# Prompt chunks of a hybrid decoder layer: K and V copies to the scalar engine, states read by row groups, and a shared centring

## What is computed

```python
u = rms_norm(h, norm_mix) @ w_in
y_ssd, y_ret, y_gla, y_lru = mixers(split(u))
h = h + concat([y_ssd, y_ret, y_gla, y_lru]) @ w_out
hn = rms_norm(h, norm_ffn)
h = h + (silu(hn @ w_gate) * (hn @ w_up)) @ w_down
```

## Time and profile before

| | |
|---|---|
| median of 3 runs | 1433.16 us (1429.13 to 1435.86) |
| the profiled execution | 1434.77 us |
| its span, first to last instruction | 1433.0 us |
| PE, share of the span busy | 97% |
| DVE | 46% |
| ACT | 34% |
| POOL | 29% |
| mean granted clock of PE | 0.984 of 2.4 GHz |

### The profile page before, as it was taken

One profiled execution on the slowest core, in us unless ns is written; L12 is line 12 of the kernel. 1 busy time (PEld: TensorE's weight loads), 2 busy tenths in 40 slices (PEclk: granted clock), 3 DMA queues, 4 the chain that ended last, 5 costly groups with the idle time before them and its releaser, 6 DMA issues.

```text
span 1433.0 us, 25769 instructions
## 1 busy us (share of the span) xinstructions
PE 1388.3 (97%) x11189; PEld 1339.7 (93%) x11189; DVE 654.6 (46%) x1280; ACT 489.6 (34%) x649; POOL 415.4 (29%) x205
## 2 busy tenths in 40 slices
PE   6998999999999999999999989999999999999996
PEld 6887888999999999999989878889999999999996
DVE  5744766364321333133756547755533223322334
ACT  5625344342221222122443263534322122222231
POOL 1100001333444444443511000014333333444441
PEclk9999999999999999999999999999999999999998
DMA  8644645223222222232446456332232223322231
GB/s 276 135 101 114 144 112 120 62 86 89 89 87 83 87 87 87 89 89 89 118 131 134 103 133 158 78 90 88 75 89 89 89 89 89 88 85 83 87 101 63
DMA packets 41345, 146.39 MB, mean 102 GB/s; under 512 B 5136, under 2 KB 6160, under 8 KB 41104
## 3 DMA queue, kind: packets, MB, share of 16 engines
q1 hardware_dynamic: 30528, 112.33, 26.6%
q0 software_dynamic: 6336, 23.07, 8.8%
q10 hardware_dynamic: 4368, 9.34, 2.1%
HBM read 136.68 MB, written 5.82 MB: 99 GB/s over the span
## 4 chain that ended last, share of the span: by engine, by line
PE 84%; DVE 7%; ACT 3%; DVEq 2%; DMA 2%; issue 1%; ACTq 1%; POOL 0%; SPq 0%
PE bank L1224 75%; DMA wl<-weights 1%; PE bank L1174 1%; PE bank L1453 1%; DMA tz<-rq 1%; PE bank L1345 1%; PE bank L1315 0%; ACT wh L403 0%; ACT wl L405 0%; PE bank L1190 0%; ACT xh L428 0%; PE bank L1459 0%; DVE h L1165 0%; PE bank L1185 0%; DVE ct L719 0%
## 5 line engine op out<-in xcount | busy, mean ns | idle before, releaser
L1224 PE MATMUL bank<-xh,wh 128*128 128x272 f32 x2208 | 653.2, 296 | 15.8 <-DVE xl L676 7.6
L1224 PE MATMUL bank<-xh,wl 128*128 128x272 f32 x2208 | 644.7, 292 | 0.0
L1224 PE MATMUL bank<-xl,wh 128*128 128x272 f32 x2208 | 641.3, 290 | 0.0
L375 POOL TENSOR_TENSOR wl<-raw,wh 128x1024 fp32r<-128x1024 f32 x157 | 377.1, 2402 | 594.4 <-ACT wh L403 578.5
L403 ACT ACTIVATE wh<-raw 128x1024 fp32r<-128x1024 f32 x199 | 210.8, 1060 | 688.4 <-PE bank L1224 665.8
L1224 PEld LDWEIGHTS bank<-xh,wh 128*128 128x128 f32 x2208 | 422.0, 191 | 23.3 <-issue 17.2
L1224 PEld LDWEIGHTS bank<-xl,wh 128*128 128x128 f32 x2208 | 422.5, 191 | 1.3 <-issue 0.5
L1224 PEld LDWEIGHTS bank<-xh,wl 128*128 128x128 f32 x2208 | 421.3, 191 | 0.0
L1143 DVE TENSOR_TENSOR tz<-bank,rs_bcast 128x272 f32<-128x272 f32 x176 | 77.5, 441 | 293.5 <-PE bank L1224 289.5
L1123 DVE TENSOR_TENSOR h<-h,bank 128x272 f32<-128x272 f32 x128 | 55.3, 436 | 215.5 <-PE bank L1224 215.5
L382 POOL DMA_DIRECT2D wl<-weights x44 | 38.1, 867 | 397.2 <-ACT wl L405 397.2
(11 more groups left out here) (360 smaller groups left out, 1790.5 us busy)
## 6 DMA issues: line engine op xcount, KB each, us to landing
raw<-weights SPq DMA_DIRECT2D x202, 512.0 KB, 3.6
wl<-weights POOLq DMA_DIRECT2D x44, 512.0 KB, 7.8
h<-x SPq DMA_DIRECT2D x4, 544.0 KB, 6.0
y<-h SPq DMA_DIRECT2D x4, 544.0 KB, 2.8
cs<-consts SPq DMA_DIRECT2D x1, 1656.5 KB, 9.3
rv<-rk ACTq DMA_DIRECT2D x8, 136.0 KB, 6.6
tz<-rq ACTq DMA_DIRECT2D x8, 136.0 KB, 4.0
S<-s_ssd ACTq DMA_DIRECT2D x2, 512.0 KB, 4.3
```

The source lines that it names most:

```text
L375: nc.gpsimd.tensor_tensor(wl[:, s, :], raw[:, s, :], wh[:, s, :].bitcast(F32), ALU.subtract).then_inc(lo_done, 1)
L1224: ins = mm(bank_, wt[:, n % RING, w], xx[:, cols], start=(i == 0 and j == 0), stop=(i == len(ks) - 1 and j == 2))
```

## The change

The masks `ssd_blocks`, `gla_blocks`, `ret_blocks` and the tile `dS` go (the table of constants loses 640 columns of 128 rows in float32). The states keep whatever K^T V has outside a head's block; PE reads only the own rows: per chunk from 1 on, four state matmuls in each mixer, of 64 x 64 tiles in SSD (before: four of 128 x 64) and retention (before: two of 128 x 128) and of 32 x 64 tiles in GLA (before: two of 128 x 128), all behind the four of V instead of between them. DVE adds K^T V from PSUM onto the state. ACT copies K of SSD, K and V of GLA, and V of retention, each with a new signal that PE's part b waits for. K of SSD is turned into M[1], V of retention into M[3], and GLA's output lies in M[2] and M[1], so `gla_a` now waits for ACT's copy of the chunk before (`gla_o`). DVE makes retention's `qt` before it waits for `ret_a`. In the centring ACT squares the two prompt halves from PSUM while DVE copies.

```diff
@@ signals
+        ssd_k, gla_kv, ret_v = (signal(n, 4) for n in ("ssd_k", "gla_kv", "ret_v"))
+        cent_mm, cent_first, cent_second, cent_out = (
+            signal(n, 1) for n in ("cent_mm", "cent_first", "cent_second", "cent_out"))
@@ scalar
                     a(D[:], M[0][:].rearrange("p (h i) -> p h i", h=4), ACT.Exp).then_inc(ssd_dx.sem, 1)
+                    a(K[:, 0:P], M[1][:, 384:512], ACT.Copy).then_inc(ssd_k.sem, 1)
+
+                def gla_a_(c):
+                    if c < SAMPLE:
+                        act.wait_ge(gla_a.sem, gla_a.at(layer, c + 1))
+                        a(V[:], M[1][:, 0:256], ACT.Copy)
+                        a(K[:, 0:P], M[1][:, 256:384], ACT.Copy).then_inc(gla_kv.sem, 1)
+                        gla_pre_(c + 1)
+
+                def ret_a_(c):
+                    if c < SAMPLE:
+                        act.wait_ge(ret_a.sem, ret_a.at(layer, c + 1))
+                        a(V[:], M[3][:, 256:512], ACT.Copy).then_inc(ret_v.sem, 1)
...
                 def ret_squares(_=None):
+                    act.wait_ge(cent_mm.sem, cent_mm.at(layer, 1))
+                    a(sq[:, 1, 0:SEQ], M[1][:], ACT.Square).then_inc(cent_second.sem, 1)
+                    act.wait_ge(cent_first.sem, cent_first.at(layer, 1))
+                    a(sq[:, 0, 0:SEQ], M[0][:], ACT.Square)
                     act.wait_ge(cent_out.sem, cent_out.at(layer, 1))
-                    squares(rv[:])
+                    a(sq[:, :, SEQ:TOK], rv[:, :, SEQ:TOK], ACT.Square).then_inc(n_sq.sem, 1)
@@ vector
-                    copy(K[:, 0:P], M[2][:, 384:512])
...
-                            stt(S_gla[:], S_gla[:], gla_last[:, c % 2, 0:1], dS[:], ALU.mult, ALU.add)
+                        new = M[3][:, 0:256]
+                        if c == 0:
+                            copy(S_gla[:], new)
+                        else:
+                            stt(S_gla[:], S_gla[:], gla_last[:, c % 2, 0:1], new, ALU.mult, ALU.add)
...
-                    copy(V[:], M[1][:, 0:256])
-                    copy(K[:, 0:P], M[1][:, 256:384])
...
                 def ret_a_(c):
                     _, off, n = CH[c]
+                    if c < SAMPLE:
+                        tt(qt[:, c % 2, :, :], rq[:, :, off:off + n], cst("ret_q").rearrange("p (t i) -> p t i", t=2), ALU.mult)
                     dve.wait_ge(ret_a.sem, ret_a.at(layer, c + 1))
...
-                    copy(V[:], M[2][:, 256:512])
-                    tt(qt[:, c % 2, :, :], rq[:, :, off:off + n], cst("ret_q").rearrange("p (t i) -> p t i", t=2), ALU.mult)
...
+                        for t in range(2):
+                            cols = slice(P * t, P * t + P)
+                            if c == 0:
+                                copy(S_ret[:, cols], M[0][:, cols])
+                            else:
+                                stt(S_ret[:, cols], S_ret[:, cols], cst("ret_last")[:, t:t + 1], M[0][:, cols],
                                     ALU.mult, ALU.add)
...
+                    copy(rv[:, 0, prompt], M[0][:]).then_inc(cent_first.sem, 1)
+                    copy(rv[:, :, sample], M[2][:, 0:2 * NS].rearrange("p (t n) -> p t n", t=2))
                     dve.drain().then_inc(cent_out.sem, 1)
+                    dve.wait_ge(cent_second.sem, cent_second.at(layer, 1))
+                    copy(rv[:, 1, prompt], M[1][:])
@@ tensor
+                    pe.wait_ge(ssd_k.sem, ssd_k.at(layer, c + 1))
                     for hd in range(4):
                         g, r = hd // 2, hd % 2
+                        mm(M[g][64 * r:64 * r + 64, 0:P], V[:, 64 * hd:64 * hd + 64], PT[:, hd, :], start=True, stop=c == 0)
+                    for hd in range(4 if c else 0):
+                        g, r = hd // 2, hd % 2
+                        rows = slice(64 * g, 64 * g + 64)
+                        mm(M[g][64 * r:64 * r + 64, 0:P], S_ssd[rows, 64 * hd:64 * hd + 64], qt[rows, c % 2, r, :],
+                           start=False, stop=True)
...
+                    if c:
+                        pe.wait_ge(gla_o.sem, gla_o.at(layer, c))
...
+                    pe.wait_ge(gla_kv.sem, gla_kv.at(layer, c + 1))
...
+                        rows = slice(32 * hd, 32 * hd + 32)
+                        mm(M[2 - t][64 * e:64 * e + 64, 0:P], S_gla[rows, 64 * hd:64 * hd + 64],
+                           qt[rows, (c + 1) % 2, 0, :], start=False, stop=True, tile_position=(32 * hd, 64 * e))
...
+                    pe.wait_ge(ret_v.sem, ret_v.at(layer, c + 1))
...
+                        rows = slice(64 * e, 64 * e + 64)
+                        mm(M[3][64 * e:64 * e + 64, t * P:(t + 1) * P], S_ret[rows, 64 * hd:64 * hd + 64],
+                           qt[rows, c % 2, t, :], start=False, stop=True, skip_group_check=True)
```

More of the change, by code:

```diff
@@ L513, in gla_b_ @@
                     for t in range(2):
-                        src = M[2][:, t * P:t * P + n] if c < SAMPLE else M[2 + t][:, 0:n]
-                        ins = a(gv[:, t, off:off + n], src, ACT.Copy)
+                        ins = a(gv[:, t, off:off + n], M[2 - t if c < SAMPLE else 2 + t][:, 0:n], ACT.Copy)
                     ins.then_inc(gla_o.sem, 1)
@@ L860, in ssd_b_ @@
                     else:
-                        tt((S_ssd if c == 0 else dS)[:], M[2][:, 0:256], cst("ssd_blocks"), ALU.mult)
-                        if c:
-                            dve.drain()
+                        if c == 0:
+                            copy(S_ssd[:], M[2][:, 0:256])
+                        else:
                             for r in range(2):
-                                new, old = (x[:].rearrange("p (g r d) -> p g r d", g=2, r=2)[:, :, r, :] for x in (dS, S_ssd))
+                                new, old = (x.rearrange("p (g r d) -> p g r d", g=2, r=2)[:, :, r, :]
+                                            for x in (M[2][:, 0:256], S_ssd[:]))
                                 stt(old, old, E[:, r, P - 1:P], new, ALU.mult, ALU.add)
@@ L1319, in ssd_a_ @@
                         mm(M[2 + g][:, 0:n], xbc[rows, 2, off:off + n], xbc[rows, 3, off:off + n], start=True, stop=True)
-                    for t in range(3):
-                        ins = turn(M[2][:, P * (t + 1):P * (t + 2)], xbc[:, t, off:off + n])
-                    ins.then_inc(ssd_a.sem, 1)
+                    for t in range(2):
+                        turn(M[2][:, P * (t + 1):P * (t + 2)], xbc[:, t, off:off + n])
+                    turn(M[1][:, 384:512], xbc[:, 2, off:off + n]).then_inc(ssd_a.sem, 1)
                 def ssd_b_(c):
@@ L1435, in ret_b_ @@
                         mm(M[3][64 * e:64 * e + 64, t * P:(t + 1) * P], V[:, 64 * hd:64 * hd + 64], PT[:, hd, :],
-                           start=True, stop=c == 0, skip_group_check=c > 0)
-                        if e and c:
-                            mm(M[3][:, t * P:(t + 1) * P], S_ret[:, t * P:(t + 1) * P], qt[:, c % 2, t, :],
-                               start=False, stop=True, skip_group_check=True)
+                           start=hd < 2, stop=c == 0, skip_group_check=True)
+                    for hd in range(4 if c else 0):
+                        t, e = hd // 2, hd % 2
+                        rows = slice(64 * e, 64 * e + 64)
+                        mm(M[3][64 * e:64 * e + 64, t * P:(t + 1) * P], S_ret[rows, 64 * hd:64 * hd + 64],
+                           qt[rows, c % 2, t, :], start=False, stop=True, skip_group_check=True)
                     for t in range(2):
```

44 lines of the change are left out of this document (10 added, 34 removed).

## The result

The kernel after took 1420.86 us (median of 6 runs, 1414.21 to 1428.54), the kernel before 1433.12 us beside it: a ratio of 0.9919, 95% interval [0.9898, 0.9941]. That is 12.3 us less where 6.9 were forecast. The profiled execution took 1419.99 us, its span is 1418.2 us and its mean granted clock 0.988 (before: 1434.77, 1433.0 and 0.984). Four executions that stood far above the others of their kernel (1457.22 and 2218.33 us of the state part alone, 1900.33 us of its repeat, 4661.1 us of the kernel before) are left out of all that follows.

The account below looks back on a forecast made before the run. PE, busy 97% of the span, bounds the kernel. Matmul groups 4.6 us, waits 1.4 and 1.3, less 0.2 for a new wait and 0.2 for nearly late copies, give 6.9: from 1433.16 to 1426.3 us, range 1421 to 1431.5.

Parts of the forecast that it names:

- GLA's V behind DVE: PE's wait at GLA's V matmuls, chunk 3 of each layer, goes whole as DVE loses copies and masks: 1.4 us.
- retention's V behind DVE: Three waits at retention's V matmuls: two fall by 0.26 us each, the third by 0.82; together 1.3 us.
- copies of ACT nearly late: Allowance for ACT's copies that land only just before PE needs them: 0.2 us off the gain.
- Row groups overlap: State matmuls in tiles differing in rows run together; groups save 0.48 us in GLA, 0.30 in retention, 0.05 in SSD.
- Rivals 1 and 3: Row groups sharing a bank don't overlap, 1429.2 us, chance 0.1; row groups don't overlap at all, 1434.4 us, chance 0.04.
- DVE's relief reaches PE: Copies and masks taken off DVE shorten PE's waits at the V matmuls: 1.4 us in GLA, 1.3 in retention.
- rival 2: DVE's relief doesn't reach PE, so only the matmuls' 4.6 us are gained: 1428.6 us; chance 0.2.
- Slot 41: Before retention's sample stage, V's copy on ACT adds 0.40 us, dS gives back 0.49; PE waits 0.2 us longer.
- GLA's chunk 0: ACT, late out of the LRU's gates, delays the copy of GLA's output; gla_a(1) waits 0.1 us a layer, bound 0.25.
- the copies and squares end just as PE arrives: In the centring, shortening copies and squares gains nothing, as PE has its dense half unit to do anyway.
- as many stretches below full clock as before: In the profile's window views, the number of stretches where PE's clock is below full stays the same.
- Rival 5: One or two slow half units of 4.71 us fall away, 1.7 us each: 1424.6 or 1422.9 us; chance 0.19.

Follow-up runs that it names:

- experiment 1: Kernel before with only the state part: row-group state matmuls behind V's, no masks, all copies on DVE, centring as before; 1428.50 us, ratio 0.9977.
- Experiment 3: Kernel before with the state matmuls only moved behind V's, still over all rows and with masks; 1430.52 us, ratio 0.9994.
- experiment 2: Kernel before with only the copies of K and V moved to ACT; state matmuls, masks, qt and centring as before; 1429.49 us, ratio 0.9986.
- experiments 1 and 9: The latter: kernel before with the state part and retention's queries made ahead of their wait, no copies moved, old centring; 1427.05 us, ratio 0.9948.
- kernel 12: kernel 8 with the copies of K and V in GLA's chunk 0 back on DVE; 1417.63 us, ratio 0.989 against the kernel before.
- Experiment 4: Kernel before with only the new centring: ACT squares the prompt halves from PSUM while DVE copies; 1431.32 us, ratio 0.9993.
- kernel 8: Kernel after with K^T V made only for the heads' own blocks, in small tiles; 1416.58 us, ratio 0.9891 against the kernel before.

## Why the prediction was right, and where its sizes were off

**The mechanisms of the sum held, and the clock, which it left out, gave 2.6 us more.** The forecast was 6.9 us; what it names sums to 7.2 in the rows of the two profiles, and the work fell by 8.4. PE's own account:

| term | forecast | measured |
|---|---|---|
| GLA's groups, 6, V to K^T V | -2.9 (0.48 each) | -3.1 (0.51) |
| retention's groups, 6 | -1.8 (0.30) | -1.9 (0.31) |
| SSD's groups, 6 | -0.3 (0.05) | -0.6 (0.10) |
| K^T V of GLA and retention, 12 | 0 | +1.2 (0.10) |
| GLA's V behind DVE | -1.4 | -1.4 |
| retention's V behind DVE | -1.3 | -1.8 |
| sample stage (L1405, now L1427) | +0.4 | -0.2 |
| `gla_a(1)` behind ACT | +0.2 | 0 |
| copies of ACT nearly late | +0.2 | +1.1 |
| centring's sums | 0 | -0.5 (0.27 each) |
| sum | -6.9 | -7.2 |
| LRU's gates behind ACT (L1345, now L1362) | 0 | -1.3 |
| GLA's scores of chunk 0 behind ACT's gates (L1370, now L1389) | 0 | +1.3 |

1. *Row groups overlap.* Shown: four state matmuls in four row groups of GLA take 0.38 us with their change of shape (845.97 to 846.35), retention's four in two pairs 0.58. Rivals 1 and 3 fall: they needed 1.2 us or more in GLA and 1.6 in retention, where 0.97 and 1.17 stand. The Trainium skill (TensorEngine Tiling (Array Packing), PSUM Pressure) says that different row tiles cannot access the same PSUM bank simultaneously. This trace doesn't bear that out where each row group writes partitions of its own, as here. But the forecast's sum ends where K^T V starts, and with row groups K^T V itself comes 0.10 us dearer in GLA and retention: 1.2 us that it put at nothing. And overlap is not where the gain comes from. Experiment 3 has all of PE's 4.4 us without any row group; the row groups earn their place by taking the masks off DVE. A rival that the prediction doesn't name, that the order is what counts, is thus the right one for PE's own part.
2. *DVE's relief reaches PE.* Shown, against rival 2, by experiments 1 and 2: the copies alone close GLA's wait for DVE, and the state part alone halves it. Retention's third wait went, and the two left are 0.3 us at the longest, behind DVE, as forecast.
3. *Slot 41.* The mechanism is shown by experiment 2, where the wait grew by 0.5 us with the copies and no unmasked state, and by experiment 1, where it fell by 0.5 without the copies. But with both it was 0.9 us, not 1.5: ACT's V copy there took 0.27 us in the chain (916.54), not 0.40, which is 0.26 of the 0.6 us for the two layers; the queries ahead gave 0.1 a layer or less (0.6 us without them, 0.4 with them in experiments 1 and 9). The term was mis-sized by 0.6 us, and the wait did not take the gain of chunk 3. The kernel after, layer 1:

```profile
916.54 0.27 ACT V L482
916.81 0.55 ACT gh_ssd L546
```

4. *GLA's chunk 0.* I had ACT's copies nearly late at 0.2 us for the whole kernel; they were late by 0.53 us in each layer. I saw that ACT comes late out of the LRU's gates, and then priced only the output copy behind it, not K's and V's in the slot ahead. The rows: PE starts `gla_a(0)` when ACT has read the last gates, after a wait of 0.67 us, and from there it needs 4.6 us to V's matmuls; ACT needs from the same moment the rest of the gates, two weight copies and V and K, 5.1 us to the landing of K.

```profile
831.53 1.08 PE L1389 MATMUL bank<-D,kz 128*32 128x128 f32 x32 [0.67 <-ACT ct L490]
```

In the profiles read, the wait at K stood only where that of 0.67 us stood before it (both layers of after, layer 1 of after again, of own blocks and of the kernel without queries), and never in the profiles without it (copies alone, without centring). In kernel 12 the first wait is there twice and the second not at all: with DVE doing that chunk it is gone. Whether the wait of 0.67 us is there goes with the clock: it stands in exactly those layers of the fourteen profiles in which PE has no slow stretch behind the LRU's gates (both layers of after, of state part alone in its first profile, of without copies and of kernel 12, and one layer of six others; none in the four left). So a stretch that falls away there gives back 0.3 us and not 1.5: in the kernel after, the two waits of 0.67 and 0.53 us take its place. The wait for `gla_o`, which I had put at 0.2, did not show in this profile, and once each at 0.2 to 1.3 us in five of the others.
5. *Centring.* The step that failed is "the copies and squares end just as PE arrives", put at nothing. Just was not early enough. The timelines (ACT and PE; before, then after; the half unit ahead ends at 250.93 and 247.18):

```profile
249.77 1.11 ACT L529 ACTIVATE Vx<-rv 128x1088 f32<-128x1088 f32 x1 [2.21 <-DVEq L1091]
...
250.94 2.17 PE L1453 MATMUL bank<-cs,Vx 128*128 128x2 f32 x20
```

```profile
245.70 0.25 ACT L567 ACTIVATE Vx<-rv 128x64 f32<-128x64 f32 x1
...
247.01 2.06 PE L1478 MATMUL bank<-cs,Vx 128*128 128x2 f32 x20
```

Before, the squares end at 250.88 and the first sum starts at 250.94, behind the half unit's end. After, they end at 245.95, 1.2 us ahead as forecast, and the first sum starts 0.17 us before the half unit ends. The chain shows no wait in either, yet 0.27 us a layer were lost. Experiment 4 shows that they belong to the centring's edit; that the start of the first sum is what makes the difference is read from these rows.
6. *Clock.* The forecast expected as many stretches below full clock as before, and named a change in their number as a sign of being wrong. They went from nine to five in the two profiles, so that step failed; in the second profile of the same kernel they are eight, and between the fourteen profiles five to eleven. Rival 5 did come on top of the forecast, by its price: three stretches of 1.5 us in the two profiles, some 2.6 us over the runs. Which edit brings it is only partly settled. The half unit behind the centring's sums ran at full clock in both layers in after (twice), without copies, without queries and with own blocks, five profiles that all have the state part and the new centring; it was slow in at least one layer in the eight that lack one of these. But it was slow again in kernel 12, which has both. So the two together make it likely, neither alone does, and nothing forces it.

The last two rows of the table were in no term. PE's wait for ACT at the LRU's gates, which the prediction put down to the recurrence of the LRU, went from 6.2 to 4.9 us, all of it in layer 1, and its length goes with how long ACT's queue is held by the issue of one DMA (last section). The other, new wait cancels it. What is left over, between 7.2 and 8.4 us, is open. In the two profiles PE's waits in the first units (for DVE at `cbuf`, for `wl` by DMA and by POOL) are 2.1 us less too, but 0.9 of that is a wait that the new slow stretch at 32 us covers, and the waits for `wl` went from 1.7 to 5.7 us between the fourteen profiles, with 3.1 and 3.8 in the two of the kernel after. So 8.4 is good to about a microsecond.

**What to carry to other kernels.** Price a group of matmuls by its changes of tile shape as well as by its columns, and up to the start of the work behind it: putting matmuls of one shape together gave all that row groups seemed to give PE. Before a copy goes to the engine that "has time", look for the one slot in which it has none, and count every copy of that slot, the moved one first. And take the clock out of the times, by span times granted clock, before judging an edit of a few us: the same code measured twice stood 3.5 us apart, and its work 0.4 us.

## What the runs showed of the hardware

- A float32 matmul of 128 columns that fills the 128 x 128 array takes 0.22 us here, start to start, where the shape does not change (order alone: 218.20 to 218.65, two of them), and two in 128 x 64 tiles side by side take the same (four of V in 0.43 us). Two full ones behind V's tiles take 0.55 us (217.65 to 218.20).
- A change of tile shape costs 0.1 to 0.2 us: V's four take 0.59 us up to the next shape for 0.43 without the change, and K^T V of 256 columns takes 0.35 us behind small tiles for 0.25 behind full ones. It is paid wherever the shape changes and moves with it. In kernel 8, GLA's group is 0.38 us shorter in the chain (layer 0, chunk 2), but the half unit behind it takes 3.20 us in place of 3.00.
- Twenty tiny matmuls of the sums took 1.90 us in the chain with the squares there 1.2 us ahead, and 2.17 with the squares done as PE arrived; the half unit of 24 behind them took 3.21 or 4.7 us.
- ACT's issue of the load of GLA's state in layer 1 took 2.15 us in the profile of before and 0.81 in that of after:

```profile
826.02 2.15 ACTq L588 DMA_DIRECT2D S<-s_gla  x1
```

```profile
819.73 0.81 ACTq L606 DMA_DIRECT2D S<-s_gla  x1
```

In layer 1 it was 0.8 in all ten profiles that have the state part, and 1.0 to 2.2 in the four that don't; in layer 0 it was 1.6 to 2.0 in those four and 0.5 to 2.1 in the ten. PE's wait at the LRU's gates is this time and 1.2 to 1.3 us more, in 27 of the 28 layers of the fourteen profiles (layer 1: 3.4 us before, 2.0 after). The 28th is layer 0 of kernel 12, where the issue just ahead of it took 2.43 us in place of 0.48, and the wait was 3.6 us. So the issues on ACT's queue stand in PE's path; what makes one short was not tried.
